# Up projection by Strassen's scheme in groups two to four of a two-layer decoder trunk

## What is computed

```python
x = layer_norm(DEEPNORM_ALPHA * x + merged @ w_out, ln1_g, ln1_b)
hdn = jnp.square(jax.nn.relu(x @ w_up))
x = layer_norm(DEEPNORM_ALPHA * x + hdn @ w_down, ln2_g, ln2_b)
```

## Time and profile before

| what | value |
|---|---|
| time, median of 3 runs | 2209.93 us (2191.13 to 2211.57) |
| profiled execution, its own time | 2206.95 us |
| its span | 2205.2 us |
| TensorE busy | 2168.7 us, 98% of the span, 16404 matmuls |
| VectorE, ScalarE, GpSimd busy | 960.0, 356.8, 1384.2 us |
| mean granted TensorE clock | 0.993 of full |

### The profile page before, as it was taken

How to read it: one execution, slowest core, us unless ns; L and a number is a source line. 1 busy time by engine, 2 the same in 40 slices (tenths; PEclk the granted TensorE clock), 3 DMA queues, 4 the chain that set the end, 5 groups by cost and what they waited for, 6 DMA issues and landing times.

```text
span 2205.2 us, 39087 instructions
## 1 busy us (share of the span) xinstructions
PE 2168.7 (98%) x16404; PEld 2123.5 (96%) x16404; DVE 960.0 (44%) x1453; ACT 356.8 (16%) x613; POOL 1384.2 (63%) x1605
## 2 busy tenths in 40 slices
PE   8999999999999999999999999999999999999997
PEld 8998999999998999999999989999999989999997
DVE  7156200542478332414691571006423892414147
ACT  3122021041022100000141210200310230000002
POOL 6644667545675776767666446665456767767673
PEclk9999999999999999999999999999999999999999
DMA  5315334235221322222223153333243222222221
GB/s 187 105 58 173 115 96 134 67 106 172 82 91 58 96 77 81 91 76 77 77 66 118 58 174 113 102 114 102 76 163 96 78 77 92 82 77 78 94 77 44
DMA packets 199906, 214.97 MB, mean 97 GB/s; under 512 B 5216, under 2 KB 192608, under 8 KB 199776
## 3 DMA queue, kind: packets, MB, share of 16 engines
q1 hardware_dynamic: 170304, 172.84, 24.9%
q10 hardware_dynamic: 29472, 40.20, 5.5%
HBM read 199.06 MB, written 13.97 MB: 97 GB/s over the span
## 4 chain that ended last, share of the span: by engine, by line
PE 94%; DVE 5%; issue 0%; ACT 0%; DMA 0%; ACTq 0%; DVEq 0%
PE gp L449 66%; PE gp L465 7%; PE gp L475 7%; PE qb L555 6%; PE gp L618 4%; PE gp L792 1%; PE gp L804 1%; PE qb L586 1%; PE gp L613 1%; DVE r L1868 1%; DVE r L1759 1%; DVE dacc L1715 0%; DVE qb L1756 0%; DVE sqacc L1744 0%; DVE x_lo L1768 0%; DVE r L1762 0%
## 5 line engine op out<-in xcount | busy, mean ns | idle before, releaser
L396 POOL TENSOR_TENSOR w_lo<-stage,w_hi 128x256 fp32r<-128x256 f32 x1264 | 1033.3, 848 | 56.2 <-ACT w_hi L1130 29.8
L393 POOL TENSOR_SCALAR w_hi<-stage 128x1024 fp32r<-128x1024 f32 (+1 forms) x316 | 336.0, 1063 | 726.3 <-PE gp L449 441.5
L449 PE MATMUL gp<-x_hi,w_hi 128*128 128x288 f32 x2176 | 468.4, 297 | 0.0
L449 PE MATMUL gp<-x_lo,w_hi 128*128 128x288 f32 x2176 | 465.4, 295 | 0.0
L449 PE MATMUL gp<-x_hi,w_lo 128*128 128x288 f32 x2176 | 465.3, 295 | 0.0
L449 PEld LDWEIGHTS gp<-x_hi,w_hi 128*128 128x128 f32 x2176 | 350.5, 189 | 2.9 <-issue 2.6
L449 PEld LDWEIGHTS gp<-x_lo,w_hi 128*128 128x128 f32 x2176 | 350.3, 189 | 0.0
L449 PEld LDWEIGHTS gp<-x_hi,w_lo 128*128 128x128 f32 x2176 | 350.3, 189 | 0.0
L449 PE MATMUL gp<-b_hi,w_hi 128*128 128x288 f32 x1408 | 304.7, 298 | 0.0
L449 PE MATMUL gp<-b_hi,w_lo 128*128 128x288 f32 x1408 | 301.4, 296 | 0.0
L449 PE MATMUL gp<-b_lo,w_hi 128*128 128x288 f32 x1408 | 301.3, 296 | 0.0
(11 more groups left out here) (237 smaller groups left out, 3105.4 us busy)
## 6 DMA issues: line engine op xcount, KB each, us to landing
stage<-in_w_in SPq DMA_DIRECT2D x62, 1024.0 KB, 5.6
stage<-in_w_up SPq DMA_DIRECT2D x32, 1024.0 KB, 5.4
stage<-in_w_down SPq DMA_DIRECT2D x32, 1024.0 KB, 5.0
stage<-in_w_ret_out SPq DMA_DIRECT2D x8, 1024.0 KB, 5.4
stage<-in_w_mem_kv SPq DMA_DIRECT2D x8, 1024.0 KB, 5.1
stage<-in_w_out SPq DMA_DIRECT2D x8, 1024.0 KB, 5.1
s_in_c<-in_ret_state ACTq DMA_DIRECT2D x8, 512.0 KB, 5.2
out_ret_sample<-s_in_c ACTq DMA_DIRECT2D x8, 512.0 KB, 3.5
```

The costliest lines, as they stand in the source:

```text
L393: nc.gpsimd.tensor_scalar(hi, raw, 1.0, 1.0, ALU.mult, ALU.mult).then_inc(hi_done, 1)
L396: ins = nc.gpsimd.tensor_tensor(lo[:, k:k + 2, :], raw[:, k:k + 2, :], hi[:, k:k + 2, :].bitcast(F32), ALU.subtract)
L449: last = mm(gp[:, 2 * (i % 2) + half, 0:HALF], w[:, i % 4, k * P:(k + 1) * P], x(k, half), start=(n == 0), stop=(n == 3 * nk - 1))
```

## The change

The first group stays as it was. In groups two to four the up projection takes two output tiles at once (a "pair", p = 0 to 3) as a 2 x 2 block product: the k dimension (1024) is halved into 4 + 4 k tiles, the pair's 256 output features into two tiles of 128, and the 576 columns into two halves of 288. It is done in seven products of quarters instead of eight (Winograd's form of Strassen's scheme). Each product is 4 k tiles by 3 terms, 12 matmuls of 128x288, into one bank of `gp`, and some are accumulated on a bank that already holds another product. Its order is the table `SEVEN`.

- Sums of x (four per k tile, `row_sums`) are made once in each layer by VectorE between the first four down tiles of the first group, with their high part by ScalarE and their low part by VectorE (`row_sums_low`).
- Sums of weight quarters are made by VectorE in the four `qb` banks (`weight_sum`), four per pair; their high parts by ScalarE, their low parts by VectorE (`sum_low`). The three quarters that are used raw get their high part from ScalarE and their low part from GpSimd (`raw_low`).
- The partial results of products 0, 2, 3 and 5 are copied out by ScalarE (`keep_part`); VectorE adds one to a bank for each of the four output quarters (`quarter_out`), and makes relu and square in one instruction for each tile (`squared`). The high part of the hidden tile is made by ScalarE, the low part by GpSimd, for the last pair by VectorE.
- TensorE waits before each product (`seven_products`), and for two k tiles together in the first down tile of these groups.
- The loops over groups are written out on all engines.

```diff
+SEVEN = ((0, 0), (1, 0), (None, 1), (None, 2), (1, 1), (None, 3), (None, 4))
...
+    def seven_free(eng, l, g, p, n):
+        if p == 0:
+            tile_is_done(eng, l, T_FF + 16 * g - 4 + n // 2)
+        else:
+            eng.wait_ge(prod_done, 7 * pair_no(l, g, p - 1) + n + 1)
...
+            for g in range(1, 4):
+                for p in range(4):
+                    raw_low(l, g, p, 0)
+                    if p >= 2:
+                        hidden_low(l, g, p - 2, 1)
+                    raw_low(l, g, p, 1)
+                    if p >= 2:
+                        hidden_low(l, g, p - 2, 0)
+                    raw_low(l, g, p, 2)
...
+                split_four(l, T_FF + 16 * g + 8, behind=(g, pair_no(l, g, 3)))
+                split_four(l, T_FF + 16 * g + 12)
...
+                pe.wait_ge(raw_split, 3 * q + 1)
+                pe.wait_ge(pair_free[0], l * (TILES // 2) + half_t + 1)
+                one(0, a, rows_of(0, 0), True)
+                pe.wait_ge(raw_split, 3 * q + 2)
+                pe.wait_ge(pair_free[1], l * (TILES // 2) + half_t + 1)
+                one(1, b, rows_of(1, 0), True)
+                pe.wait_ge(t_split, 4 * q + 1)
+                one(2, c, rows_sum(0), True)
+                pe.wait_ge(t_split, 4 * q + 2)
+                pe.wait_ge(part_in, 4 * q + 1)
+                one(3, a, rows_sum(1), False)
+                pe.wait_ge(raw_split, 3 * q + 3)
+                pe.wait_ge(part_in, 4 * q + 2)
+                one(4, c, rows_sum(3), False)
+                pe.wait_ge(t_split, 4 * q + 3)
+                pe.wait_ge(part_in, 4 * q + 3)
+                one(5, a, rows_sum(2), False)
+                pe.wait_ge(t_split, 4 * q + 4)
+                pe.wait_ge(quarter_made, 4 * q + 1)
+                one(6, b, rows_of(1, 1), True)
...
-                for i in range(4 * first, 8):
-                    product(l, g * 16 + T_FF + i, g * 8 + (T_FF + i) // 2, i, *X)
+                else:
+                    if g == 1:
+                        pe.wait_ge(s_split, l * 4 + 4)
+                    for p in range(4):
+                        seven_products(g, p)
...
+                    keep_part(q, 3, a, 2)
+                    if more:
+                        seven_high(g, p + 1, 3)
+                        seven_high(g, p + 1, 4)
+                    keep_part(q, 5, a, 3)
+                    if more:
+                        seven_high(g, p + 1, 5)
+                    hidden_high(g, p, 1)
+                    if more:
+                        seven_high(g, p + 1, 6)
...
+            def row_sums(k):
+                for i in range(2):
+                    ins = vec_.tensor_tensor(x_sum[:, i, :], x_hi[:, 4 * i + k, :].bitcast(F32),
+                                             x_lo[:, 4 * i + k, :].bitcast(F32), ALU.add)
+                link(ins)
+                (a11, a12), (a21, a22) = ([x_sum[:, i, COLS[h]] for i in range(2)] for h in range(2))
+                link(vec_.tensor_tensor(s_raw[:, 0, :], a21, a22, ALU.add))
+                vec_.tensor_tensor(s_raw[:, 2, :], a11, a21, ALU.subtract)
+                link(vec_.tensor_tensor(s_raw[:, 1, :], s_raw[:, 0, :], a11, ALU.subtract))
+                vec_.tensor_tensor(s_raw[:, 3, :], a12, s_raw[:, 1, :], ALU.subtract).then_inc(s_made, 1)
+
+            def row_sums_low(k):
+                dve.wait_ge(s_high, l * 4 + k + 1)
+                vec_.tensor_tensor(s_lo[:, :, k, :], s_raw[:, :, :], s_hi[:, :, k, :].bitcast(F32),
+                                   ALU.subtract).then_inc(s_split, 1)
...
+            def up_projection(g):
+                for p in range(4):
+                    more = p < 3
+                    if more:
+                        weight_sum(g, p + 1, 1)
+                    quarter_out(g, p, 0)
+                    if more:
+                        sum_low(g, p + 1, 1)
+                        weight_sum(g, p + 1, 2)
+                        weight_sum(g, p + 1, 3)
+                        sum_low(g, p + 1, 2)
+                        weight_sum(g, p + 1, 4)
+                    quarter_out(g, p, 1)
+                    quarter_out(g, p, 2)
+                    squared(p, 1)
+                    if more:
+                        sum_low(g, p + 1, 3)
+                    quarter_out(g, p, 3)
+                    squared(p, 0)
+                    if more:
+                        sum_low(g, p + 1, 4)
...
+                        down(g, m)
+                        if g == 0 and m < 4:
+                            row_sums(m)
+                            row_sums_low(m)
```

More of the change, by code:

```diff
@@ L424, in _ @@
                 pool.sem_inc(split_done, 2)
-        with pool.Fori(0, DEPTH - 1) as l:
-            layer(l, False)
-        layer(DEPTH - 1, True)
+        for l in range(DEPTH):
+            layer(l, l == DEPTH - 1)
         pool.wait_ge(last_mean_in, 1)
@@ L947, in _, with seven_products, rows_of, rows_sum @@
             closing_four(l, T_WO + 4, 0, *M)
+            def seven_products(g, p):
+                q, half_t = pair_no(l, g, p), (T_FF + 16 * g + 2 * p) // 2
+                a, b, c = (0, 3)[p % 2], 2, 1
+                def rows_of(k_half, half):
+                    return [[x[:, 4 * k_half + k, COLS[half]] for k in range(4)] for x in (x_hi, x_lo)]
+                def rows_sum(i):
+                    return [[x[:, i, k, :] for k in range(4)] for x in (s_hi, s_lo)]
+                def one(n, bank, rows, start):
+                    hi, lo = rows
+                    for k in range(4):
+                        for m, (w, x) in enumerate(((w_hi, hi), (w_hi, lo), (w_lo, hi))):
+                            last = mm(gp[:, bank, 0:HALF], seven_slot(w, n)[:, k, :], x[k], start=(start and k == m == 0),
+                                      stop=(k == 3 and m == 2), **({} if start else {"skip_group_check": True}))
+                    last.then_inc(prod_done, 1)
+                pe.wait_ge(raw_split, 3 * q + 1)
[18 more added lines that the diff above has]
+                one(6, b, rows_of(1, 1), True)
+                pe.sem_inc(tile_done, 2)
             def mlp(g, first=False, last=False):
@@ L962, in _ @@
             mlp(0, first=True)
-            with pe.Fori(1, 3) as g:
-                mlp(g)
-            mlp(3, last=True)
+            for g in range(1, 4):
+                mlp(g, last=(g == 3))
             if l == DEPTH - 1:
@@ L1348, in _ @@
                 act_fn(relu4[:, j, :], gp[:, j, 0:HALF], ACT.Relu).then_inc(relu_in, 1)
-                act.wait_ge(relu_in, l * 32 + j + 1)
+                act.wait_ge(relu_in, l * 8 + j + 1)
                 act.sem_inc(pair_free[j // 2], 1)
@@ L1905, in _, with hidden @@
-            base = steps[0] + group(0, steps[0], first=True)
-            with dve.Fori(1, 3) as g:
-                per = group(g, g * 16 + (base - 16))
-                assert per == 16
-            steps[0] = base + 2 * per
-            steps[0] += group(3, steps[0], last=True)
+            def hidden(i, t, cols):
+                link(vec_.tensor_tensor(t, t, t, ALU.mult))
+                link(vec_.tensor_copy(b_hi[:, i, cols], t))
+                return vec_.tensor_tensor(b_lo[:, i, cols], t, b_hi[:, i, cols].bitcast(F32), ALU.subtract)
@@ new lines, in down @@
+            def down(g, m):
+                tile_is_done(dve, l, g * 16 + T_FF + 8 + m)
+                vec_.tensor_tensor(halves(r[:, m, :]), halves(r[:, m, :]), pair(m % 2),
+                                   ALU.add).then_inc(pair_free[m % 2], 1)
+            def row_sums(k):
[8 more added lines that the diff above has]
+                vec_.tensor_tensor(s_raw[:, 3, :], a12, s_raw[:, 1, :], ALU.subtract).then_inc(s_made, 1)
@@ new lines, in _ @@
+            for j in range(4):
+                dve.wait_ge(relu_a, l * 4 + j + 1)
+                hidden(j, relu4[:, j, :], COLS[0]).then_inc(hidden_a, 1)
+            for j in range(4):
+                dve.wait_ge(relu_in, l * 8 + j + 1)
+                hidden(j, relu4[:, j, :], COLS[1]).then_inc(hid_ready, 1)
+            for i in range(4, 8):
+                dve.wait_ge(relu_in, l * 8 + i + 1)
+                hidden(i, relu[:, i % 2, :], slice(0, N)).then_inc(hid_ready, 1)
+            dve.wait_ge(r_ready, l * 8 + 8)
```

201 lines of the change are left out of this document (165 added, 36 removed).

## The result

The changed kernel takes **2178.66 us** (median of 8 runs, 2177.86 to 2180.43) beside 2209.73 us for the kernel before on the same chip (median of 8, 2191.13 to 2211.57). The ratio is 0.9883 with a 95% interval of 0.986 to 0.9905: faster by 1.2%. The profiled execution took 2177.93 us, its span 2176.1, where before it was 2206.95 and 2205.2. So 29.1 us of span are gone, of the 38.4 us that the removed matmuls were worth.

A forecast was written before the change was run, and what follows sets the result against it. TensorE, busy 98% of the span, was taken as the bound, so only fewer or shorter matmuls help. 2206.95 - 38.4 (matmuls) + 10.0 (row sums) + 5.4 (transitions) = 2184.0 us, given as 2185; range 2168 to 2211.

The forecast's parts named there:

- Removed matmuls, 38.4 us: Up projection, groups two to four: 24 pairs with 12 matmuls fewer each, 288 at 133.3 ns, save 38.4 us.
- the side at "40": Upper side of the saving from removed matmuls: 40 us, with 132.6 ns for the new matmuls.
- The row sums, +10.0 us: First group's down projection: 9.0 us rounds exceed the 6.4 us tile, TensorE loses 5.0 us a layer; between 0 and 16.4.
- GpSimd would go on at 3.87 us per tile throughout: First group's down projection: GpSimd works 3.87 of each 6.4 us, so five of VectorE's seven instructions meet it.
- The transitions, +5.4 us: Between pairs inside groups: the next pair's product 1 waits for the last quarter, 18 times 0.3 us; between 0 and 18.
- the square of 1.18 us: Chain from product 5 to the last quarter: VectorE's square takes 1.18 us beside GpSimd's last raw low part; chain 3.4 us.
- The forecast's fork ("with a short square it is in time"): Next pair's product 1: 0.2 us late as reckoned, in time with a short square, 0.6 late with one of 1.6.
- What was put at nothing: No cost from first-pair weights, group ends, 1 MB loads or written-out loops; no waits for `part` or the sums' low parts.
- Everything hides: Rival: row-sum rounds under 7.75 us and short squares, so only the 38.4 us saving shows: 2168.6 us; chance 0.17.
- Dear PSUM writes: Rival: VectorE's weight sums into PSUM take 1.3 us, not 0.69, 2.0 us at each transition: 2214.6 us; chance 0.10.
- Taking turns wholly: Rival: VectorE and GpSimd fully exclude each other, rounds of 10.7 us, 0.6 us at each transition: 2203 us; chance 0.17.
- The clock: Rival: row-sum stalls drop TensorE's clock to half for three tiles in each layer, costing 38 us: 2222 us; chance 0.06.

The follow-up runs named there:

- Run 4: The changed kernel with the last of each pair's seven products done twice, 12 matmuls more in each of 24 pairs: 2217.99 us.
- run 1: The changed kernel with VectorE's row sums spread behind seven of the eight residual additions of the first group's down projection, nothing left out: 2169.42 us.
- Runs 2 and 3: The changed kernel with one more VectorE square in each pair but a group's last: ahead of the last output quarter (2) 2191.69 us, behind it (3) 2178.35 us.
- run 5: The kernel before with its loops over groups written out on four engines, nothing else: 2201.17 us beside 2209.1, ratio 0.9985.
- Run 9: The changed kernel with row sums spread over the first group, plus a TensorE wait before the first down tile of each group with pairs: 2175.89 us.
- run 6: The changed kernel with the two additions into `x_sum` made twice in each row-sum round: 2186.77 us.

## Why the prediction was right, and where it was not

Forecast: 2185.0 us, by the profiled execution's own time 2184.0. Measured: 2178.66, and 2177.93. It lies in the range and on the side that was given the most (under 2188, 0.44); the sum was 6.1 us too high. The step from 2184.0 to 2185 follows from nothing: by the 3 us that the text names it would be 2187. Term by term:

- **Removed matmuls, 38.4 us.** The pairs save 12.80 - 11.17 = 1.63 us each, 39.1 in 24. The 0.7 more is the spacing of the one-half form, 132.9 instead of 133.3 ns, the side at "40" of the text. Run 4 put the matmuls back and got 39.3 us. Another 1.3 us is not the work of the change: 384 matmuls of layer 1 ran at 130.0 ns (49.91 us, not 51.2), as the kernel before does in some executions.
- **The row sums, +10.0 us.** Measured 11.1 by the two stages and by the blocks of run 1, 9.2 by its median. The mechanism is the one of the text: two-operand instructions that meet GpSimd, the round over 6.4 us, TensorE waiting for `r`. But that the total is near is luck, two errors that cancel. The round was 9.97, 9.66, 8.54 and 6.56 us in layer 1, a sum of 34.7 where 4 x 9.0 = 36.0 was taken, and the waits are 7.0 us where 10.0 were forecast, one tile earlier than forecast. The step that failed is that GpSimd would go on at 3.87 us per tile throughout, a reading from group two. In the first group it is behind: in the kernel before, too, it works without a wait until 745.62 us (first row below). So it was busy nearly all of the first round, and hardly at all in the last, because its weights for the group were made and the next needed ScalarE. The other 4.1 us are the clock (3.4) and what a stop costs beyond its wait; the first was a rival and not a term, and the second was in no part of the text.
- **The transitions, +5.4 us: the term that was mis-sized.** It measured 0. The chain from product 5's end to the last quarter took 2.9 us, not 3.4, with 3.2 available. The step is the square of 1.18 us, "GpSimd's last raw low part runs then". GpSimd's part had ended at 812.28 us and the square began at 812.71. Of 48 squares 42 took 0.76 us, and the six long ones are one in each group's last pair, where no product waits for them. Runs 2 and 3 show that the chain is the right one: 0.76 us more on it makes all 18 transitions wait, 0.76 us beside it none. The forecast's fork ("with a short square it is in time") came out on the other branch.
- **What was put at nothing.** No wait for `part`, for the low parts of the sums or at the second down tile of a group is in the list of TensorE's waits. Loops written out change nothing that can be measured (run 5).

The first row here is GpSimd's first wait in that stretch of the kernel before. The others are from timelines of the changed kernel: such a long square, in the first of the six groups, and two costs that only bounds could give:

```profile
747.87 1.04 POOL L393 TENSOR_SCALAR w_hi<-stage 128x1024 fp32r<-128x1024 f32 x1 [2.24 <-PE gp L449]
...
835.05 1.17 DVE L2119 SCALAR_TENSOR_TENSOR relu_odd<-relu_odd 128x576 f32<-128x576 f32 x1
...
799.66 0.69 DVE L2092 TENSOR_TENSOR qb<-stage,qb 128x512 f32<-128x512 f32 x1
...
809.10 1.44 POOL L456 TENSOR_TENSOR b_lo<-relu,b_hi 128x576 fp32r<-128x576 f32 x1
```

VectorE writes a sum of 512 columns into PSUM in 0.69 us, as was taken from the nearest row, and GpSimd's hidden low part takes 1.44 us (about 1.5).

**The rivals.** *Everything hides* (2168.6) was right on the pairs and wrong on the row sums; the spread version, in which it is right on both, took 2169.42. *Dear PSUM writes* (2214.6) falls with the 0.69 us; its own working is loose, since 3 x (1.3 - 0.69) is 1.8 and not 2.0 us, and its 2214.6, like the clock's 2222, is booked as slower though both lie within the 1% of no change that the text sets. *Taking turns wholly* (2203) falls: a round of 10.7 us was needed and a pair that waits 0.6, and the rounds are 6.6 to 10.0. In the first round VectorE's seven instructions lost 8.0 - 4.7 = 3.3 us beside 9.8 us of GpSimd. From 741.57 to 747.89 us, 6.3 us, VectorE did six instructions worth 3.3 us alone, and GpSimd work worth 4.7 (by its durations in the earlier trace rows): less than their sum, 8.0. The Trainium skill (SBUF — State Buffer, Who interferes with whom) has the two engines excluding one another for whole instructions. These rows do not agree: the engines lengthen one another, and neither stands for all of the other's work. *The clock* (2222) did fall, but for some 3.5 us in each layer and not for three tiles of 6.4: 3.4 us in all instead of 38.

Against the kernel before the gain depends on which of its levels one meets: 12 us on a run near 2191, 22 on one near 2201, 31 on one near 2210. The changed kernel has little of this scatter (2177.86 to 2180.43), since in its profile only the 384 matmuls of layer 1 ahead of the first wait had the short spacing among the long stretches, and the tiles behind the seven products always 133.3 ns.

The sum of the parts in the profiled executions: -39.1 for the pairs, +11.1 for the first group, -1.3 for its spacing, -29.3 us in all; the two blocks differ by 29.6 (697.6 and 668.0 us), and the spans, with what lies outside the blocks, by 29.1.

## What to carry to other kernels

Where TensorE is the bound, a scheme with fewer products is worth the number of matmuls removed times their spacing, to within 2% here, and what decides is where its preparations stand on the other engines. The same seven instructions cost 11 us in one piece between two residual additions and left a single wait of 0.2 us when they were spread over the tiles, and the same square cost 13 us ahead of the instruction that frees a bank and nothing behind it. So follow the chain to each release of a buffer, keep on it only what the release needs, and place the rest behind it in pieces shorter than the slack of one tile.

## What the runs showed of the hardware

- **Matmuls of 288 columns with the same weights for two halves in turn ran at 130.0 or at 133.3 ns each.** In a long stretch without a stop the spacing stayed the same throughout (2616 matmuls in 340.08 or in 348.79 us), at a granted clock of full speed in both. Which of the two it was differed between the two layers of one execution (run 5) and, to judge by the levels of the times, from execution to execution of one program. One half at a time ran at 132.5 to 133.1 ns in every stretch of the feed-forward blocks without a stop. What sets the spacing stays open. Run 9 shows that a stop of 1 us does not bring the short one behind the seven products, and the changed kernel that it can end at one: 130.0 ns up to the wait of 1.93 us, 133.3 behind it.
- **A short stop costs more than its wait.** A wait of 0.45 us lengthened the pair by 0.66 (run 2), and behind a wait of 1.03 us the stage was 0.26 longer (run 9). 0.16 us of it is the overlap of two matmuls that is lost (0.29 us long, 0.13 apart).
- **The granted clock fell behind some waits of TensorE and not behind others.** In layer 1 of the changed kernel it stayed at 1.00 behind the wait of 1.93 us at 761.43, and was 0.50 for some 3.5 us behind the one of 1.91 at 769.97. In layer 2 it stayed at 1.00 behind a wait of 0.52 us and was 0.50, again for some 3.5 us, behind the next, of 2.68. In run 6 a wait of 4.38 us ended at 765.28; the clock was 0.73 in the window before, with TensorE idle, and 0.50 up to 771 us.
- **VectorE and GpSimd lengthen one another.** One instruction of 288 columns with two SBUF operands took 0.46 us with GpSimd idle and 0.87 to 1.30 beside it, and four of GpSimd's low parts took from 2.82 up to 4.45 us.
